# The first pass's rows of an expert layer, turned by a one-hot product instead of a gather

## The chip, the cores and the metric

The kernel runs on one core of one Trainium2 chip. The metric is the device time of one execution in microseconds (us); all arrays are float32 in HBM when it starts. Its engines are TensorE (PE), VectorE (DVE), ScalarE (ACT), GpSimd (POOL) and SyncE (SP, which here only issues DMAs). They run their own instruction streams and meet through semaphores.

## The reference

One inference step of a backbone with two layers over 384 tokens (128 of a prompt, 256 of a sample) of width 1024. Each layer has a mixer and a mixture of 16 experts with 256 hidden columns, of which each token uses two:

```python
scores = jax.nn.sigmoid((t @ router_w).astype(jnp.float32))
sel = scores + router_b.astype(jnp.float32)
grp = sel.reshape(n, N_GROUPS, EXP_PER_GROUP)
gscore = lax.top_k(grp, TOP_K)[0].sum(-1)
g_idx = jnp.argmax(gscore, axis=-1)
...
combine = jnp.sum(jax.nn.one_hot(e_idx, N_EXPERTS, dtype=jnp.float32) * wts[..., None], axis=1).astype(t.dtype)
hid = jax.nn.silu(jnp.einsum('td,edf->tef', t, w1)) * jnp.einsum('td,edf->tef', t, w3)
hid = hid * combine[:, :, None]
return jnp.einsum('tef,efd->td', hid, w2).reshape(bsz, s, d)
```

The mixers (convolution and latent attention in layer 0, spatial gating in layer 1), the adaLN modulation and the norms lie before and between the two expert layers and are not touched.

## The kernel before

**The expert layer.** Every expert j has a fixed stretch of places (`PLACE_AT[j]`, 96, 64 or 32 of them); a token that chooses j takes the next free place of it. The 1152 places are worked off in nine passes of 128. For a pass p the rows of h of its 128 tokens must stand turned (columns of h on the partitions) in `h_slotT`. Then TensorE multiplies them with w1 and w3 of the pass's experts ("up", two halves of 32 products, L1691), ScalarE takes the silu (L725), VectorE multiplies (`gate`), TensorE turns the hidden rows (L1730) and multiplies with w2 ("down", L1706). Down's result goes through y_slot to a table in HBM, from which it is gathered back at the layer's end (L547).

**How a pass got its rows.** In `dispatch` TensorE turns h into rows (L1604), ScalarE copies them to `h_rows` on chip (L764) and stores them in HBM as `h_all` (L767). From the router's scores VectorE makes each token's place in each expert (`place`), compares it with the place numbers 1, 2, ... and so gets a one-hot matrix `chosen` (token by place, fp16; `choose`). TensorE multiplies it with the token numbers and gets the list of tokens by place: `tokens` (L1626), for passes 0 to 2 in `dispatch` and for 3 to 8 later, since the experts from the sixth on are first sorted by their load. VectorE casts the list to the integers `table` (L1102). GpSimd gathers the 128 rows of a pass from `h_all` by the table (`fetch`, L536) into one of two slots of `h_slot`; TensorE turns them (`turn_h`, L1672 and L1676, four transposes each), and ScalarE and VectorE copy the two halves to `h_slotT` (`copy_h`, L721 and L1244). The slots of `h_slot` lie over `h_rows`.

**What sets the order.** Each engine's stream is written out by hand; nothing is scheduled. VectorE's order in `place` is: one-hots of the first four experts and the fifth's stretch of places, the table's cast, the sorting of the experts (`sort_experts`, `order_experts`, which releases the load of the sixth expert's weights on SyncE's queue), the weights of the tokens (`shares`), the modulation columns (`ada`, on which TensorE's experts wait, since it empties a PSUM bank), then in `experts_routed` the later one-hots (`later_places`). TensorE's order in `experts_routed` is:

```python
turn_h(0)
pe.wait_ge(s_chosen, (1 + len(RUNS)) * (l + 1))
tokens(bank[7], *TABLES[1]).then_inc(s_table, 1)
up(0, range(KD // 2))
turn_h(1)
up(0, range(KD // 2, KD))
```

and then the turned weights of the last pass (L1719) and the loop over the passes, in which pass p+1's up stands around pass p's hidden rows and ahead of its down, and `turn_h(p + 2)` between. Weights of six experts are held at a time; SyncE loads an expert's w1 and w3 when the up products of the expert six before it are done, and its w2 after that one's down. PSUM's eight banks are given to the products of `PRODUCTS` in turn.

## Time and profile before

| | us |
|---|---|
| median of 3 runs | 750.0 (749.42 to 752.58) |
| profiled execution | 752.46 |
| its span, first to last instruction | 750.4 |
| TensorE busy | 672.7 |
| VectorE busy | 258.2 |
| ScalarE busy | 159.1 |
| GpSimd busy | 32.5 |

The span is the time from the first instruction of the program to the last; 2.06 us of the execution lie around it. The two expert layers follow at about 262 and 577 us of the span with their dispatch, up of pass 0 starts at 286 and 601, and up of the last pass ends at about 394 and 710. Over the whole span the 16 DMA engines move 285 GB/s; while the passes run it is mostly over 400.

### The profile page before, as it was taken

What the parts mean: (1) busy time and instruction counts of PE and PEld (TensorE: products, weight loads), DVE (VectorE), ACT (ScalarE), POOL (GpSimd) and SP (SyncE); (2) the same over time, 40 slices, a digit from 0 to 9 for tenths busy, and PEclk for the clock granted to TensorE, in tenths of its full rate; (3) what the DMA queues carried; (4) which work ended last, traced back from release to release, by engine and by line L of the source; (5) the groups of instructions that cost most, each with busy time, mean ns of one, the idle gap of its engine ahead of it and who ended that gap; (6) DMA issues with size and microseconds to landing.
All of it is one profiled execution on the core that took longest, in us unless ns stands there. A gap on an engine that the chain in (4) does not pass through costs nothing.

```text
span 750.4 us, 11306 instructions
## 1 busy us (share of the span) xinstructions
PE 672.7 (90%) x4744; PEld 345.0 (46%) x4744; DVE 258.2 (34%) x600; ACT 159.1 (21%) x316; POOL 32.5 (4%) x88
## 2 busy tenths in 40 slices
PE   4699999999989858999977799999998499999884
PEld 2555555557755523333323545556654333333242
DVE  0504678366511473121101620020425711211027
ACT  2301000253411231111111430131013311111023
POOL 2000000000000011000002000000000010010020
PEclk9999999999999987999999999999999889999898
DMA  9996030769974378899997895423745778999852
GB/s 368 381 425 273 33 140 1 317 274 424 424 307 167 131 298 299 324 401 418 425 428 283 324 397 227 183 111 121 314 169 217 290 299 309 405 424 424 352 197 84
DMA packets 27556, 213.63 MB, mean 285 GB/s; under 512 B 2768, under 2 KB 6640, under 8 KB 15856
## 3 DMA queue, kind: packets, MB, share of 16 engines
q1 hardware_dynamic: 17568, 182.06, 59.7%
q0 software_dynamic: 4320, 15.73, 6.0%
q10 hardware_dynamic: 5616, 15.09, 5.1%
q8 instruction: 39, 0.64, 0.3%
q14 instruction: 13, 0.11, 0.0%
HBM read 199.62 MB, written 13.25 MB: 284 GB/s over the span
## 4 chain that ended last, share of the span: by engine, by line
PE 77%; DVE 9%; DMA 8%; issue 2%; ACT 2%; POOL 1%; SPq 0%; POOLq 0%; DVEq 0%; ACTq 0%
PE bank L1447 29%; PE bank L1691 17%; PE bank L1706 8%; PE bank L1784 6%; DMA ring<-in_ada_w 3%; PE bank L1381 2%; DVE work L844 2%; PE bank L1500 2%; DMA state<-y_slots,index 2%; PE bank L1593 2%; DVE xT L847 2%; DMA work<-h_all,table 2%; DVE state L888 1%; PE bank L1672 1%; PE bank L1392 1%
## 5 line engine op out<-in xcount | busy, mean ns | idle before, releaser
L1447 PE MATMUL bank<-state,ring 128*128 128x384 f32 x416 | 136.1, 487 | 1.2 <-ACT state L614 1.2
L1691 PE MATMUL bank<-ring,work 128*32 128x512 f32 x896 | 110.2, 636 | 7.4 <-issue 7.4
L1447 PEld LDWEIGHTS bank<-state,ring 128*128 128x128 f32 x416 | 78.3, 190 | 54.9 <-issue 2.1
L1447 PE MATMUL bank<-work,ring 128*128 128x384 f32 x256 | 83.8, 489 | 0.3 <-DVE work L844 0.3
L1447 PEld LDWEIGHTS bank<-work,ring 128*128 128x128 f32 x256 | 48.6, 191 | 35.1 <-DVE work L844 1.3
L1691 PEld LDWEIGHTS bank<-ring,work 128*32 128x32 f32 x896 | 28.8, 116 | 73.6 <-issue 73.5
L1706 PE MATMUL bank<-ring,work 128*32 128x512 f32 x448 | 50.9, 595 | 2.6 <-ACT work L734 2.6
L1244 DVE COPY work<-bank 128x512 f32<-128x512 f32 x18 | 12.4, 691 | 111.6 <-PE bank L1676 111.6
L847 DVE SCALAR_TENSOR_TENSOR xT<-bank,mod,xT 128x128 f32<-128x128 f32 x64 | 22.5, 411 | 68.4 <-PE bank L1447 67.2
L1784 PE MATMUL bank<-ring,state 128*128 128x512 f32 x96 | 43.3, 612 | 2.4 <-ACT state L614 2.4
L536 POOL DMA_INDIRECT work<-h_all,table x18 | 17.1, 951 | 591.0 <-DMA h_all<-work 455.1
L596 ACT ACTIVATE state<-xT 128x384 f32<-128x384 f32 x40 | 20.6, 522 | 99.2 <-DVE xT L847 88.1
L1418 PE MATMUL bank<-state,share 128*128 128x384 f32 x58 | 22.6, 548 | 10.3 <-ACT state L596 10.3
L1784 PEld LDWEIGHTS bank<-ring,state 128*128 128x128 f32 x96 | 18.7, 196 | 25.7 <-issue 25.2
L1268 DVE COPY work<-bank 128x512 f32<-128x512 f32 x18 | 12.4, 692 | 50.4 <-PE bank L1706 50.4
L1691 PE MATMUL bank<-work 128*32 128x512 f32 x160 | 28.9, 594 | 0.0
L1691 PE MATMUL bank<-state,work 128*32 128x512 f32 x96 | 28.9, 594 | 0.0
L1706 PEld LDWEIGHTS bank<-ring,work 128*32 128x32 f32 x448 | 13.3, 109 | 31.0 <-issue 28.0
L847 DVE SCALAR_TENSOR_TENSOR work<-ring,csil,work 128x768 f32<-128x768 f32 x28 | 26.3, 1011 | 0.0
L1381 PE MATMUL bank<-ring,csil 128*32 128x128 f32 x704 | 22.3, 280 | 4.1 <-DMA ring<-in_ada_w 4.1
L844 DVE TENSOR_TENSOR mod<-bank,smalls 128x8 f32<-128x8 f32 (+1 forms) x32 | 3.8, 158 | 63.3 <-PE bank L1400 63.1
L1672 PE MATMUL bank<-smalls,work 128*128 128x128 f32 x72 | 12.7, 302 | 14.2 <-DMA work<-h_all,table 7.7
(211 smaller groups left out, 724.1 us busy)
## 6 DMA issues: line engine op xcount, KB each, us to landing
ring<-in_moe SPq DMA_DIRECT2D x24, 2048.0 KB, 10.0
ring<-in_ada_w SPq DMA_DIRECT2D x12, 3072.0 KB, 15.1
ring<-in_moe SPq DMA_DIRECT2D x24, 1024.0 KB, 17.9
work<-in_ada_w SPq DMA_DIRECT2D x3, 3072.0 KB, 10.1
work<-in_moe SPq DMA_DIRECT2D x4, 2048.0 KB, 11.6
state<-in_moe SPq DMA_DIRECT2D x4, 2048.0 KB, 14.5
y_slots<-work ACTq DMA_DIRECT2D x16, 512.0 KB, 9.8
ring<-in_gm_in SPq DMA_DIRECT2D x4, 2048.0 KB, 9.0
```

The source lines that it names most:

```text
L536: pool.indirect_dma_start(h_slot[:, p % 2, :], None, h_all, bass.IndirectOffsetOnAxis(ap=table[:, l, p:p + 1], axis=0))\
L596: act.activation(sq[:, k % 4, :], xT[:, k, :], ACT.Square).then_inc(s_sq, 1)
L844: return dve.tensor_tensor(o, x, y, op)
L847: return dve.scalar_tensor_tensor(out=o, in0=x, scalar=s, in1=y, op0=op0, op1=op1)
L1381: mm = pe.matmul(ps[32 * g:32 * g + 32, 0:P], csil[:, k, :], w[:, k, g * P:g * P + P], start=(k == 0), stop=(k == KD - 1))
L1418: mm = pe.matmul(ps[:, 0:T], share[:, n, :], sq[:, sq_at[0] % 4, :], start=(k == 0), stop=(k == tiles - 1))
L1447: mm = pe.matmul(ps[:, 0:T], w[:, k, j * P:j * P + P], x[:, k, :], start=(k == 0), stop=(k == KD - 1))
L1500: mm = pe.matmul(ps[:, 0:T], w_q[:, k, h * P:h * P + P], q_a[:, k, :], start=(k == 0), stop=(k == NQ - 1))
L1672: tr = pe.transpose(bank[2][:, k * P:k * P + P], h_slot[:, b, k * P:k * P + P], ident[:, :])
L1691: mm = pe.matmul(bank[p % 2][rows, :], h_slotT[:, p % 2, k * P + BLOCK * n:k * P + BLOCK * n + BLOCK], held(place_of(e))[:, k * 512:k * 51 ...
L1706: mm = pe.matmul(bank[4 + half][rows, :], hiddenT[:, p % 2, c * P + BLOCK * n:c * P + BLOCK * n + BLOCK], held(place_of(e))[:, at_:at_ + 5 ...
L1784: mm = pe.matmul(ps[:, :], hT[:, k, t * P:t * P + P], w[:, k, :], start=(k == 0), stop=(k == KD - 1))
```

## The change

Pass 0 no longer gathers. VectorE makes a second one-hot matrix for its 128 places, in float32 and on the space of `last_w` (`choose_first`: 96 places of expert 0, 32 of expert 1). TensorE multiplies the rows that still stand in `h_rows` with it (`first_rows`): for each 128 columns of h three products (one for 128 tokens), which give the pass's rows already turned. The eight blocks are made in two halves of 12 products, "hot" 0 and 1, with the first table's products between them, which now are for passes 1 and 2 only. ScalarE copies the first half to `h_slotT`, VectorE the second (`copy_first`, behind the order of the experts, with the table's cast). `h_slotT`'s two slots change places, since slot 0 lies over `h_rows`. The gathers begin with pass 1, and the first waits also for the second half of the products. Up of pass 0 stands ahead of `turn_h(1)` with nothing before it, the later table's products follow pass 0's up, and the last pass's weights are turned after pass 1's up. On VectorE pass 0's gate comes ahead of the later table's cast and the last weights.

```diff
 KEPT = [j for j in range(NE) if PLACE_AT[j] >= STORED]
-TABLES = ((0, PLACE_AT[FIXED] // P), (PLACE_AT[FIXED] // P, PASSES))
+TABLES = ((1, PLACE_AT[FIXED] // P), (PLACE_AT[FIXED] // P, PASSES))
 RUNS = [(4, 1), (5, 2), (7, 1), (8, 8)]
...
     return ([("ada_row", HEAD_ADA[l]), ("router", l), ("logits", l)] + [("h_row", l, t, c) for t in range(NT) for c in range(2)]
-            + [("ada_t", HEAD_ADA[l]), ("slots", l), ("table", l, 0)])
+            + [("ada_t", HEAD_ADA[l]), ("slots", l), ("hot", l, 0), ("table", l, 0), ("hot", l, 1)])
...
         s_kept = carve(NT * len(KEPT))
+        first_hot = last_w
         spare = work[:, work.shape[1] - SLOT:work.shape[1]]
...
                     pool.wait_ge(taken[bank_of(key)[0]], takes(key))
+                    b, turn = bank_of(("hot", l, 1))
+                    pool.wait_ge(full[b], turn + 1)
                 if p == TABLES[1][0]:
                     pool.wait_ge(s_later, l + 1)
-                if p >= 2:
-                    pool.wait_ge(s_turn1[l], p - 1)
+                if p >= 3:
+                    pool.wait_ge(s_turn1[l], p - 2)
                 pool.indirect_dma_start(h_slot[:, p % 2, :], None, h_all,
...
                 pool.wait_ge(s_hstored, 16 * NT * (l + 1))
-                for p in range(PASSES):
+                for p in range(1, PASSES):
                     fetch(l, p)
...
-                act.wait_ge(s_turn0[l], p + 1)
-                act.activation(h_slotT[:, p % 2, 0:512], bank[2][:, :], ACT.Identity).then_inc(s_copy0[l], 1)
+                act.wait_ge(s_turn0[l], p)
+                act.activation(h_slotT[:, (p + 1) % 2, 0:512], bank[2][:, :], ACT.Identity).then_inc(s_copy0[l], 1)
...
             def experts_routed(l):
-                for p in range(2):
-                    copy_h(l, p)
+                take(act.activation(h_slotT[:, 1, 0:512], product("hot", l, 0)[:, :], ACT.Identity), "hot", l, 0)
+                copy_h(l, 1)
                 silus(l, 0)
...
-            def tokens(l):
+            def choose_first(l):
+
+                own = three(s_tmp)
+                for j in range(NE):
+                    if PLACE_AT[j] < P:
+                        first, n = PLACE_AT[j], min(CAPS[j], P - PLACE_AT[j])
+                        places = place_no[:, 0:n].rearrange("p (a n) -> p a n", a=1).to_broadcast([P, NT, n])
+                        tt(first_hot[:, :, first:first + n], places, own[:, :, j:j + 1].to_broadcast([P, NT, n]),
+                           ALU.is_equal).then_inc(s_hot, 1)
+
+            def copy_first(l):
...
                 take(dve.tensor_copy(table[:, l, first:last], product("table", l, 0)[:, 0:last - first]), "table", l, 0)
+                take(dve.tensor_copy(h_slotT[:, 1, 512:D], product("hot", l, 1)[:, :]), "hot", l, 1)
...
                 take(dve.tensor_copy(s_place[:, :], ps[:, 0:NT * NE + NE]), "slots", l)
+                choose_first(l)
                 choose(l, 0, three(s_tmp), (0, 4))
...
                 dve.wait_ge(s_caps, 2 * NE + 1 + SORTED)
-                tokens(l)
                 sort_experts(l)
                 order_experts(l)
+                copy_first(l)
                 shares(l)
...
                 later_places(l)
-                copy_h(l, 0)
+                copy_h(l, 1)
+                gate(l, 0)
                 later_tokens(l)
                 last_weights(l)
-                copy_h(l, 1)
-                gate(l, 0)
-                last_weights_turned(l)
                 for p in range(PASSES):
...
                         copy_h(l, p + 2)
+                    if p == 0:
+                        last_weights_turned(l)
                     if p + 1 < PASSES:
...
+                for t in range(NT):
+                    for c in range(2):
+                        emptied(("h_row", l, t, c))
+                pe.wait_ge(s_hot, 2 * (l + 1))
+                first_rows(l, 0)
                 pe.wait_ge(s_chosen, (1 + len(RUNS)) * l + 1)
                 closed(tokens(opened("table", l, 0), *TABLES[0]), "table", l, 0)
+                first_rows(l, 1)
+
+            def first_rows(l, c):
+
+                ps = opened("hot", l, c)
+                for i in range(4):
+                    for t in range(NT):
+                        k = 4 * c + i
+                        mm = pe.matmul(ps[:, i * P:i * P + P], h_rows[:, t, k * P:k * P + P], first_hot[:, t, :],
+                                       start=(t == 0), stop=(t == NT - 1))
+                closed(mm, "hot", l, c)
...
                     b = p % 2
-                    pe.wait_ge(s_h[l][b], 16 * (p // 2 + 1))
-                    wait(pe, s_copy0[l], p)
+                    pe.wait_ge(s_h[l][b], 16 * ((p + 1) // 2))
+                    wait(pe, s_copy0[l], p - 1)
                     for k in range(4):
...
                     tr.then_inc(s_turn0[l], 1)
-                    wait(pe, s_copy1[l], p)
+                    wait(pe, s_copy1[l], p - 1)
                     for k in range(4, 8):
...
                             pe.wait_ge(ring_full[place_of(e)], 16 * (HOME["moe", (l, e)][1] + 1))
-                        pe.wait_ge(s_copy0[l], p + 1)
+                        if p == 0:
+                            emptied(("hot", l, 0))
+                            emptied(("hot", l, 1))
+                        else:
+                            pe.wait_ge(s_copy0[l], p)
                         wait(pe, s_hid[l], p - 1)
-                    if 4 in tiles:
-                        pe.wait_ge(s_copy1[l], p + 1)
+                    if 4 in tiles and p > 0:
+                        pe.wait_ge(s_copy1[l], p)
                     for k in tiles:
...
                             rows = slice(BLOCK * n, BLOCK * n + BLOCK)
-                            mm = pe.matmul(bank[p % 2][rows, :], h_slotT[:, p % 2, k * P + BLOCK * n:k * P + BLOCK * n + BLOCK],
+                            mm = pe.matmul(bank[p % 2][rows, :], h_slotT[:, (p + 1) % 2, k * P + BLOCK * n:k * P + BLOCK * n + BLOCK],
                                            held(place_of(e))[:, k * 512:k * 512 + 512],
...
-                turn_h(0)
-                pe.wait_ge(s_chosen, (1 + len(RUNS)) * (l + 1))
-                tokens(bank[7], *TABLES[1]).then_inc(s_table, 1)
                 up(0, range(KD // 2))
...
                 up(0, range(KD // 2, KD))
-                pe.wait_ge(s_w8, len(KEPT) * (l + 1))
-                for t in range(NT):
-                    tr = pe.transpose(bank[7][:, P + t * P:P + t * P + P], last_w[:, t, :], ident[:, :])
-                tr.then_inc(s_w8t, 1)
+                pe.wait_ge(s_chosen, (1 + len(RUNS)) * (l + 1))
+                tokens(bank[7], *TABLES[1]).then_inc(s_table, 1)
...
                         up(p + 1, range(KD // 2, KD))
+                    if p == 0:
+                        pe.wait_ge(s_w8, len(KEPT) * (l + 1))
+                        for t in range(NT):
+                            tr = pe.transpose(bank[7][:, P + t * P:P + t * P + P], last_w[:, t, :], ident[:, :])
+                        tr.then_inc(s_w8t, 1)
                     if p + 2 < PASSES:
...
```

The rows below are of the built programs, with the semaphores that an instruction waits for. First TensorE in layer 0, from the first table's products to the second half of pass 0's up, before. `work` is the space in which `h_rows`, `h_slot`, `h_slotT` and the one-hots lie, `smalls` holds the constants, the identity for a transpose and the place numbers among them, `ring` the weights:

```order
L1626 MATMUL bank<-token_h,work 128x1 [waits bank_taken5,chosen_ready]
L1626 MATMUL bank<-token_h,work 128x1 x8
L1672 MATMUL bank<-smalls,work 128x128 [waits bank_taken2,bank_taken3,bank_taken1,bank_taken4,bank_taken0,h_loaded0_0,bank_taken7,bank_taken6]
L1672 MATMUL bank<-smalls,work 128x128 x3
L1676 MATMUL bank<-smalls,work 128x128 x4
L1626 MATMUL bank<-token_h,work 128x1 [waits chosen_ready]
L1626 MATMUL bank<-token_h,work 128x1 x17
L1691 MATMUL bank<-ring,work 32x512 [waits h_copied00,ring_full2,ring_full1]
L1691 MATMUL bank<-ring,work 32x512 x15
L1672 MATMUL bank<-smalls,work 128x128 [waits h_copied00,h_loaded0_1]
L1672 MATMUL bank<-smalls,work 128x128 x3
L1676 MATMUL bank<-smalls,work 128x128 [waits h_copied10]
```

The same place now; L1649 is `first_rows`, L1657 `tokens`, L1726 up, L1703 and L1707 `turn_h`:

```order
L1649 MATMUL bank<-work 128x128 [waits bank_taken1,bank_taken2,bank_taken0,first_places,bank_taken7,bank_taken5,bank_taken6]
L1649 MATMUL bank<-work 128x128 x11
L1657 MATMUL bank<-token_h,work 128x1 [waits bank_taken6,chosen_ready]
L1657 MATMUL bank<-token_h,work 128x1 x5
L1649 MATMUL bank<-work 128x128 [waits bank_taken7]
L1649 MATMUL bank<-work 128x128 x11
L1726 MATMUL bank<-ring,work 32x512 [waits ring_full1,bank_taken4,ring_full2,bank_taken3,bank_taken5,bank_taken2,bank_taken7,bank_taken1,bank_taken0]
L1726 MATMUL bank<-ring,work 32x512 x15
L1703 MATMUL bank<-smalls,work 128x128 [waits h_loaded0_1]
L1703 MATMUL bank<-smalls,work 128x128 x3
L1707 MATMUL bank<-smalls,work 128x128 x4
L1726 MATMUL bank<-ring,work 32x512 x16
```

Up of pass 0 (first with `ring_full`) waited for the copy of a gathered half (`h_copied00`), and now waits for PSUM banks to be emptied (`bank_taken5` and `bank_taken7` are the two halves, `bank_taken3` the modulation). `turn_h(0)` is gone; the eighteen products of the later table have moved behind up.

VectorE in layer 0 from the places of the tokens to the sorting of the experts, before:

```order
L847 SCALAR_TENSOR_TENSOR s_tmp<-bank,s_top 128x48 [waits bank_full4,vector_step]
L1150 COPY s_place<-bank 128x64 [waits vector_step]
L844 TENSOR_TENSOR work<-smalls,s_tmp 128x3x384
L1102 CAST table<-bank 128x3 [waits bank_full5,caps_set,bank_taken4]
L847 SCALAR_TENSOR_TENSOR s_key<-s_place,smalls 128x11
```

And now:

```order
L851 SCALAR_TENSOR_TENSOR s_tmp<-bank,s_top 128x48 [waits bank_full4,vector_step]
L1164 COPY s_place<-bank 128x64 [waits vector_step]
L848 TENSOR_TENSOR work<-smalls,s_tmp 128x3x96
L848 TENSOR_TENSOR work<-smalls,s_tmp 128x3x32
L848 TENSOR_TENSOR work<-smalls,s_tmp 128x3x384
L851 SCALAR_TENSOR_TENSOR s_key<-s_place,smalls 128x11 [waits caps_set,bank_taken4]
```

The two comparisons of 96 and 32 places are new; the table's cast with its wait for TensorE has left this place.

VectorE from the order of the experts to the modulation, before:

```order
L1143 TENSOR_SCALAR order<-order 128x11 [waits vector_step]
L1144 CAST order_i<-order 128x11 [waits vector_step]
L844 TENSOR_TENSOR s_score<-s_score,s_top 128x48
L1084 TENSOR_REDUCE s_den<-s_score 128x3 [waits vector_step]
L1085 RECIPROCAL s_den<-s_den 128x3 [waits vector_step]
L844 TENSOR_TENSOR combine<-s_score,s_den 128x48 [waits vector_step]
L844 TENSOR_TENSOR work<-s_tmp,work 128x363 [waits combine_ready]
L1160 TENSOR_REDUCE work<-work 128x33 [waits vector_step]
L844 TENSOR_TENSOR mod<-bank,smalls 128x8 [waits bank_full3,vector_step]
L844 TENSOR_TENSOR mod<-bank,smalls 128x4
L844 TENSOR_TENSOR mod<-bank,mod 128x4 [waits vector_step]
```

And now:

```order
L1157 TENSOR_SCALAR order<-order 128x11 [waits vector_step]
L1158 CAST order_i<-order 128x11 [waits vector_step]
L1115 CAST table<-bank 128x2 [waits bank_full6]
L1116 COPY work<-bank 128x512 [waits bank_full7]
L848 TENSOR_TENSOR s_score<-s_score,s_top 128x48
L1088 TENSOR_REDUCE s_den<-s_score 128x3 [waits vector_step]
L1089 RECIPROCAL s_den<-s_den 128x3 [waits vector_step]
L848 TENSOR_TENSOR combine<-s_score,s_den 128x48 [waits vector_step]
L848 TENSOR_TENSOR work<-s_tmp,work 128x363 [waits vector_step]
L1175 TENSOR_REDUCE work<-work 128x33 [waits vector_step]
L848 TENSOR_TENSOR mod<-bank,smalls 128x8 [waits bank_full3,vector_step]
L848 TENSOR_TENSOR mod<-bank,smalls 128x4
```

The cast and the copy of the second half (L1116, 512 columns) stand between the order of the experts and the weights of the tokens, each with a wait for TensorE (`bank_full6`, `bank_full7`).

## Rows read from the trace of the kernel before

**Rows 1.** The page, first part: busy us, share of the span, instructions.

```profile
PE 672.7 (90%) x4744; PEld 345.0 (46%) x4744; DVE 258.2 (34%) x600; ACT 159.1 (21%) x316; POOL 32.5 (4%) x88
```

**Rows 2.** Chain of waits, layer 0: start us, us, what the time went to.

```profile
274.72 4.18 DMA h_all<-work
...
280.56 11.55 DMA work<-h_all,table
292.15 0.66 PE bank L1672 x4
293.24 3.57 PE bank L1691 x32
...
381.20 3.79 issue
```

**Rows 3.** Chain of waits, layer 1.

```profile
597.94 2.77 DVE work L844 x4
600.76 0.64 PE bank L1626 x18
601.40 6.25 PE bank L1691 x32
...
608.67 3.57 PE bank L1691 x32
...
696.63 3.64 issue
```

**Rows 4.** VectorE timeline, layer 0: start us, us, instruction, idle before and releaser.

```profile
275.04 1.35 DVE L844 TENSOR_TENSOR work<-smalls,s_tmp 128x1152 f16<-128x1152 f32 x1
276.99 0.16 DVE L1102 CAST table<-bank 128x3 uint32<-128x3 f32 x1 [0.59 <-PE bank L1626]
...
280.26 0.17 DVE L1144 CAST order_i<-order 128x11 int32<-128x11 f32 x1
...
282.67 0.16 DVE L844 TENSOR_TENSOR mod<-bank,mod 128x4 f32<-128x4 f32 x1
282.87 0.46 DVE L844 TENSOR_TENSOR work<-smalls,s_tmp 128x288 f16<-128x288 f32 x1
...
285.78 0.69 DVE L1244 COPY work<-bank 128x512 f32<-128x512 f32 x1 [0.15 <-PE bank L1676]
```

**Rows 5.** TensorE timeline, layer 0.

```profile
283.81 1.09 PE L1672 MATMUL bank<-smalls,work 128*128 128x128 f32 x4 [6.96 <-DMA work<-h_all,table]
...
286.25 5.14 PE L1691 MATMUL bank<-ring,work 128*32 128x512 f32 x32
...
296.75 0.55 PE L1719 MATMUL bank<-smalls,work 128*128 128x128 f32 x3
```

**Rows 6.** Groups of TensorE: count, busy us, mean ns, idle before.

```profile
L1796 PE MATMUL bank<-work 128*128 128x128 f32 x48 | 5.5, 275 | 0.0
```

**Rows 7.** Stretches: us, busy of PE, PEld, DVE, ACT, POOL, granted clock, DMA share, GB/s.

```profile
275.00:276.00 1.00, 0.00 (x0) 0.00 (x0) 1.00 (x2) 0.00 (x0) 0.00 (x0) 0.84 0.75 307
...
289.00:290.00 1.00, 1.00 (x16) 0.19 (x10) 0.00 (x0) 0.00 (x0) 0.00 (x0) 0.83 0.82 344
...
593.00:594.00 1.00, 0.00 (x0) 0.00 (x0) 0.89 (x6) 0.00 (x0) 0.87 (x1) 0.56 0.00 0
...
606.00:607.00 1.00, 1.00 (x8) 0.19 (x4) 0.00 (x0) 0.00 (x0) 0.00 (x0) 0.61 0.97 406
```

**Rows 8.** Timelines of GpSimd in layer 1 and of SyncE's queue in both.

```profile
594.37 0.94 POOL L536 DMA_INDIRECT work<-h_all,table  x1 [0.30 <-issue]
...
281.48 0.36 SPq L459 DMA_DIRECT2D state<-in_moe  x1
...
596.31 0.35 SPq L459 DMA_DIRECT2D state<-in_moe  x1
```

**Rows 9.** Line L536, the gathers of rows of h: from issue to landing.

```profile
DMA to landing us min/median/max: 4.0/10.5/12.8
```

**Rows 10.** DMA issues, stretch 594.3 to 594.6: count, median us to landing.

```profile
work<-h_all,table POOLq DMA_INDIRECT x1, 5.0
```

14 lines of the change are left out of this document (7 added, 7 removed).

## Prediction

> **What bounds the kernel now.** The page's first part is read first: TensorE is busy for nine tenths of the span, and no other engine for more than half [rows 1]. So time is won only where TensorE waits, or where it runs at its lower clock. The chain of waits then shows where it waits near the change. In layer 0 the chain leaves TensorE altogether: the rows of h are stored, the gather of pass 1 is on its way for 11.55 us, and TensorE turns these rows at 292.15; the second half of pass 0's up products starts at 293.24 [rows 2]. In layer 1 the chain goes through VectorE's later one-hot rows, the later table's products and the first half of up, which takes 6.25 us; the second half starts at 608.67 [rows 3]. These two starts, 293.24 and 608.67, are my anchors: behind them pass follows pass without a wait, up to one stop of 3.79 and 3.64 us before the last pass's up products [rows 2, 3]. The chain calls that stop "issue", since a wait for weights is not in its names; the reader should see that a stop ended by a load hides a loss of a few tenths ahead of it, but gives a gain on only if the loads start earlier too.
>
> **VectorE.** Two one-hots of 128x288 and 128x96 stand ahead of the comparison over 1152 columns. The nearest row is the one of 288 columns, 0.46 us [rows 4]; since instructions of this engine overlap a little I put the two at 0.4 and 0.2 (together between 0.5 and 0.9). So the large comparison ends 0.6 later. The wait of 0.59 before the table's cast goes, because the cast moves behind the sorting [rows 4]. The two cancel, and the order of the experts is ready as before (280.43: the cast at 280.26 and its 0.17). Behind it the cast and a new copy of 128x512 come in; the copy of the same shape took 0.69 [rows 4]. The modulation, which ended at 282.83 (282.67 and 0.16), and with it the release of TensorE, come 0.7 later.
>
> **TensorE ahead of the copy.** 24 products of 128x128 by 128 columns are new, 12 in each half. At the full clock 48 products of this shape took 5.5, or 0.115 each [rows 6]: 1.4 for a half. At the lower clock four transposes of the shape took 1.09 [rows 5]: 3.3 at most for a half. In layer 0 the clock fell at 275.7 (0.84 as the mean of 275 to 276, between 1.00 and 0.50, the levels of 2.4 and 1.2 GHz) [rows 7], just where the first half begins (first one-hots at 275.04 + 0.6 = 275.7). I take the first half at the lower level: 275.7 + 3.3 = 279.0; the six table products are put at 0.3 (eighteen took 0.64 [rows 3]). By then the engine has worked for 3.6 us without a pause. The clock rose at 289.3, 5.5 us after work began at 283.81 [rows 5, 7], and in layer 1 at 606.8, 6.0 after 600.76 [rows 3, 7]. So the second half lies between 1.4 and 3.3; I take 1.6, and it ends at 280.9. The copy, which could start at 280.5, waits 0.4 (bounds 0 and 2.1). In layer 1 the clock fell only at 593.1 [rows 7], the products start at 590.7, all are done by 594, and the copy (order ready 595.5) waits for nothing.
> On the price of such a product the Trainium skill differs: "FP8 and Floating Point Precision", section "TensorE Precision Notes", says that true FP32 takes four passes through the array. At 128 columns and 2.4 GHz that is an estimate of 0.21 each, 2.6 a half, and the sum would be about 1 us smaller; the row of 0.115 says about half of that, and it decides.
>
> **The first half of up.** It no longer waits for a gather, nor for the later table. It starts when the modulation is done: 282.83 + 0.7 + 0.4, and a little for the release, 284.0; in layer 1 597.9 + 0.7 + 0.4 = 599.0. The same 32 products take 3.6 at the full level (at 293.24), twice that at half, and took 5.14 and 6.25 here [rows 5, 3]. TensorE stands still from 281 to 284 and from 594 to 599, so I take 6.3 in both: ends 290.3 and 605.3. Turning pass 1 takes 1.1 (292.15 to 293.24). The anchors become 291.4 and 606.4: 1.8 and 2.3 earlier.
>
> **The gather of pass 1.** On POOL's queue it is now the first. It waits for the table's cast, for the second half of the products (its slot lies over the rows they read) and for the stored rows: 280.9 to 281.1 in layer 0 instead of 280.56, 595.8 instead of 594.37 [rows 2, 8]. The load of expert 5 is issued at 281.48 and 596.31 as before [rows 8], since the order of the experts does not move. A gather took from 4.0 to 12.8 [rows 9]; the one issued 1.9 ahead of a load took 5.0 [rows 8, 10], the one 0.9 ahead took 11.55 [rows 2, 8], both behind pass 0's. With nothing ahead of it I take 7: 288 and 603, before 290.3 and 605.3, so no wait. At 12.8 it would be 293.9 and 608.6.
>
> **What moves behind the anchor.** The later table's products, 0.64 [rows 3], now stand after pass 0's up; the three transposes of the last weights, 0.55 [rows 5], move from there to behind pass 1's up. Pass 1's end is 0.1 later against the anchor, later passes 0.6. The stop before the last pass takes up part of it, as long as the loads that end it are released by pass 1 and not by later ones: between 0.1 and 0.6 a layer, I take 0.2. The gather of pass 3 waits for the later table behind pass 0's gate, about 5 us after the anchor instead of 1, and is needed two passes on, at some 12 us each (88 us lie between 293.24 and 381.20, seven and a half passes): hidden even at 12.8. The last weights are needed one pass later than they are ready. SP's queue waits for the same events. ScalarE's new copy of 128x512 lies under the second half of the products.
>
> **Sum.** 1.8 + 2.3 - 0.4 = 3.7 us. The profiled execution took 752.46 (span 750.4 and 2.06 around it) and would take 748.8. The three timed runs have their median at 750.0, so the forecast is 746.3. The bound between "faster" and "no change" is 0.5%, which is 3.75 us and all that a measurement can tell: the forecast stands on it.
>
> **Rivals.**
> A, the clock stays up. If the new products raise the level early and the pause of 3 us does not take it back, the first half of up takes 3.6 in layer 0: it ends 287.6, then waits perhaps 0.4 for the gather, and the anchor is 289.1 instead of 291.4, 2.3 better; in layer 1, with a pause of 5 us and the clock lost after shorter activity, half of that at best. Time 743 to 744. For it: the level in layer 0 rose after 5.5 us of work. Against it: in both layers up began at the lower level, the rise came only at 289.3 and 606.8 [rows 7].
> B, the gather is late though issued first. If the load's data reach the DMA engines while the gather's last rows are still waiting, it takes 11.5 as in layer 0 before: it lands at 292.5 and 607.3, the anchors are 293.5 and 608.3, about as before, and the 0.2 to 0.6 a layer remains. Time 750. For it: its lead over the load shrinks to 0.4 and 0.5 us, where 0.9 was too little before. Against: pass 0's gather, issued just before it, then stood ahead of it in the queue, and now nothing does.
> Here the Trainium skill speaks against the change: "DMA: Bandwidth & Descriptors", section "Queues, rings and completion order", has each DMA engine go round between the queues packet by packet, so that a lead in time protects only what has already moved. The 11.55 agrees with it.
> C, slower. If the second half of the products runs at the lower level to its end, it is done at 282.6, after the load of expert 5 has been issued (281.48): this is the point from which it decides. The copy and the modulation on VectorE wait 2.1, up starts at 285.7, and the gather is issued at 282.7 behind the load and takes 11.5 to 12.8: 294.2 to 295.5. The anchor comes at 295.3 to 296.6, a loss of 2.1 to 3.4. Should the clock fall early in layer 1 too, its products end at 597.6 behind the load at 596.31, and it loses 1.7 to 2.9. Both layers: 754 to 756; layer 0 alone, with layer 1 as forecast: about 751.
> D, the change does what it says at the start, but the stop before the last pass grows by it. If the loads that end the stop leave the DMA engines when they did before, nothing is won: 750. Against: these loads are released by the ends of up, which move with the anchor.
>
> **Chances and range.** The forecast 0.46 (own range 744.5 to 748.5, for the clock's start may cost 1 us either way in each layer), A 0.17, B 0.20, C 0.12 (both layers 0.07), D 0.05. Faster by over 0.5% (below 746.25): half of the forecast and A, with a little from elsewhere: 0.42. Slower (above 753.75): C in both layers, and what runs differ by: 0.11. Within: 0.47. The range leaves out the worse C and the best of A: 742.5 to 752.
>
> **What would show it.** Right: no gather for pass 0; the products from 275.7 and done by 281; up's first half starting near 284 and 599 without a wait for a gather; the second half at 291.4 and 606.4; a stop of about 3.5 before the last pass. The chain in layer 0 should go through VectorE and no longer through a gather. Wrong: a TensorE wait for the DMA before turning pass 1 (B or C); a VectorE wait before the new copy of more than 1 us (C); a stop before the last pass grown by 2 us (D). A level of 1.00 during the first half of up would show A.

## The result, and the profile after

The changed kernel is slower. Its median is 753.27 us (748.84 to 756.47, 20 runs), that of the kernel before, on the same chips, 749.7 us (746.79 to 752.78, 20 runs); the ratio is 1.0059, with a 95% interval of 1.0042 to 1.0075. The forecast was 746.3 in a range of 742.5 to 752.0. The profiled execution took 754.07 us, its span is 752.3 (before: 752.46 and 750.4).

The first fence is the chain of waits of the changed kernel in layer 0, with the stop ahead of the last pass as its last row; columns as in [rows 2].

```profile
276.11 5.46 PE bank L1649 x24
281.71 2.90 PE bank L1649 x24
284.63 0.70 DVE work L1116
285.34 2.71 issue
288.05 5.34 PE bank L1726 x32
...
294.41 3.57 PE bank L1726 x32
...
383.06 3.70 issue
```

The gather of 11.55 us is gone from the chain, as forecast. In its place stand the two halves of the products (L1649), VectorE's copy (L1116) and 2.71 us in which the chain names no releaser. The second half of pass 0's up begins at 294.41; it was 293.24 [rows 2], and 291.4 was forecast.

The next fence is the same view in layer 1, with the stop ahead of the last pass and the end of the layer.

```profile
590.69 2.92 PE bank L1649 x24
593.74 2.80 PE bank L1649 x24
596.60 0.70 issue
597.30 8.92 DMA work<-h_all,table
...
607.36 3.57 PE bank L1726 x32
...
696.08 3.74 issue
...
721.09 1.25 PE bank L1793 x3
722.34 2.60 issue
724.95 6.43 PE bank L1793 x13
```

Here the second half begins 1.3 us earlier than before (607.36 against 608.67 [rows 3]; 606.4 was forecast), and the gather that the change was to hide is on the chain. Counted from the routing's places (the products ahead of the one-hots, which start at 274.44 and 589.02, before at 274.25 and 589.25), the two starts moved by +1.0 and -1.1 us in these executions, where -1.8 and -2.3 were forecast. At the end of the layer TensorE adds the last pass's results (L1793: eight products, which leave sixteen records). It stops after three of the sixteen, for 2.60 us. In the kernel before these sixteen run without a stop, as its timeline has it:

```profile
721.68 7.09 PE L1758 MATMUL bank<-work 128*128 128x384 f32 x16 [2.40 <-issue]
```

VectorE's timeline of the changed kernel in layer 0 answers [rows 4]; the last column is the idle time before and its releaser.

```profile
280.22 0.17 DVE L1158 CAST order_i<-order 128x11 int32<-128x11 f32 x1
281.75 0.16 DVE L1115 CAST table<-bank 128x2 uint32<-128x2 f32 x1 [1.35 <-PE bank L1657]
284.63 0.69 DVE L1116 COPY work<-bank 128x512 f32<-128x512 f32 x1 [2.73 <-PE bank L1649]
...
287.57 0.16 DVE L848 TENSOR_TENSOR mod<-bank,mod 128x4 f32<-128x4 f32 x1
```

The copy stood still for 2.73 us, where 0.4 was forecast and 2.1 was the upper bound. The modulation behind it ends at 287.73; TensorE begins pass 0's up at 288.05. So I read the 2.71 us of "issue" as a wait for VectorE; the run mod_hold below shows it.

The group of the products in the whole program answers [rows 6] (count, busy us, mean ns, idle before), and four stretches answer [rows 7] (the granted clock is the number behind the five busy times).

```profile
L1649 PE MATMUL bank<-work 128*128 128x128 f32 x96 | 14.3, 316 | 2.7 <-DVE work L848 2.7
```

```profile
280.00:281.00 1.00, 1.00 (x7) 1.00 (x6) 0.35 (x2) 0.00 (x0) 0.00 (x0) 0.50 0.00 0
282.00:283.00 1.00, 1.00 (x12) 1.00 (x11) 0.00 (x0) 0.20 (x1) 0.00 (x0) 1.00 1.06 229
289.00:290.00 1.00, 1.00 (x8) 0.27 (x4) 1.00 (x1) 0.00 (x0) 0.00 (x0) 0.50 0.96 406
...
600.00:601.00 1.00, 1.00 (x8) 0.38 (x12) 1.00 (x4) 0.00 (x0) 0.00 (x0) 0.50 1.11 475
```

The change adds 24 products in each of two layers, 48 in all, and the trace has 96 records of them: such a product of float32 leaves two. (So a half of up, called 32 products ahead of the prediction, is 16 products and 32 records: the rows of the built program have 1 and 15 of them, the chain x32. A transpose leaves one: 4 in the program, x4 in the chain.) In layer 0 the first half ran at 0.50 (1.2 GHz), the second at 1.00 (2.4 GHz), and after the pause up's first half began at 0.50 again, in layer 1 too.

Last, the transfers: the issue of expert 5's load on SyncE's queue in layer 0 (it did not move, [rows 8]), then GpSimd's issue of the first gather in layer 0 and in layer 1.

```profile
281.45 0.36 SPq L461 DMA_DIRECT2D state<-in_moe  x1
```

```profile
285.48 1.08 POOL L540 DMA_INDIRECT work<-h_all,table  x1 [280.75 <-PE bank L1649]
...
597.30 0.94 POOL L540 DMA_INDIRECT work<-h_all,table  x1 [183.11 <-PE bank L1649]
```

The gather was to lead the load by 0.4 us; it follows it by 4.0 us in layer 0 and, with the load at 595.78, by 1.5 us in layer 1.

### The profile page after: what moved, and what is told of

Its sections match the earlier page's. It is cut to its first block, busy times and chain, and to the rows that moved or that the text cites. A ratio compares the mean times of both kernels' runs of the same rounds, so it can differ in the third digit from the quotient of the medians.

```text
span 752.3 us, 11460 instructions
## 1 busy us (share of the span) xinstructions
PE 678.7 (90%) x4818; PEld 354.6 (47%) x4818; DVE 259.3 (34%) x604; ACT 158.9 (21%) x316; POOL 30.5 (4%) x86
## 4 chain that ended last, share of the span: by engine, by line
PE 80%; DVE 8%; DMA 6%; issue 3%; ACT 2%; POOL 1%; SPq 0%; DVEq 0%; ACTq 0%; POOLq 0%
PE bank L1462 28%; PE bank L1726 17%; PE bank L1741 8%; PE bank L1819 6%; DMA ring<-in_ada_w 3%; PE bank L1396 2%; PE bank L1515 2%; PE bank L1649 2%; DVE work L848 2%; PE bank L1608 2%; DVE xT L851 2%; DVE state L892 1%; PE bank L1703 1%; DMA work<-h_all,table 1%; PE bank L1564 1%
## 5 line engine op out<-in xcount | busy, mean ns | idle before, releaser
L1726 PE MATMUL bank<-ring,work 128*32 128x512 f32 x896 | 109.1, 630 | 14.6 <-issue 14.5
L1726 PEld LDWEIGHTS bank<-ring,work 128*32 128x32 f32 x896 | 29.6, 115 | 79.4 <-issue 79.4
L1819 PE MATMUL bank<-ring,state 128*128 128x512 f32 x96 | 41.6, 593 | 2.4 <-ACT state L618 2.4
L540 POOL DMA_INDIRECT work<-h_all,table x16 | 15.1, 946 | 591.8 <-PE bank L1649 463.9
L1726 PE MATMUL bank<-work 128*32 128x512 f32 x160 | 28.9, 594 | 0.0
L1726 PE MATMUL bank<-state,work 128*32 128x512 f32 x96 | 28.9, 594 | 0.0
L892 DVE RECIPROCAL state<-state 128x384 f32<-128x384 f32 x6 | 15.3, 2552 | 29.3 <-ACT state L608 29.3
## 6 DMA issues: line engine op xcount, KB each, us to landing
state<-in_moe SPq DMA_DIRECT2D x4, 2048.0 KB, 12.8
y_slots<-work ACTq DMA_DIRECT2D x16, 512.0 KB, 10.3
```

The source lines that it names most:

```text
L540: pool.indirect_dma_start(h_slot[:, p % 2, :], None, h_all, bass.IndirectOffsetOnAxis(ap=table[:, l, p:p + 1], axis=0))\
L892: step(dve.reciprocal(rms, rms))
L1726: mm = pe.matmul(bank[p % 2][rows, :], h_slotT[:, (p + 1) % 2, k * P + BLOCK * n:k * P + BLOCK * n + BLOCK], held(place_of(e))[:, k * 512: ...
L1819: mm = pe.matmul(ps[:, :], hT[:, k, t * P:t * P + P], w[:, k, :], start=(k == 0), stop=(k == KD - 1))
```

## The experiments

Sixteen runs were made, of fifteen kernels (a_pad48r is a_pad48 once more), each timed beside the kernel before. The table that follows is worked out from TensorE's records of each profiled execution. "Front" is the time from the first product of the routing's places (274.25 before) to the first of pass 2's up, in layers 0 and 1; it holds what the change does at a layer's start. "Tail" is the time in layer 1 from the end of the last up to the end of those sixteen records. "Sum" is what front and tail together differ from the kernel before. "Timed" is the ratio less one, with half its 95% interval, times 749 us.

```
kernel          front 0  front 1   tail    sum     timed us
before            34.97    35.39  18.23      0            0
changed           36.32    34.70  21.41   +3.8   +4.4 +-1.2
third             35.92    35.64  18.20   +1.2   +2.5 +-1.9
act_copy          39.63    38.03  18.06   +7.1   +9.1 +-2.2
hold              35.29    33.28  20.27   +0.3   +1.6 +-2.0
mod_hold          33.08    33.19  20.89   -1.4   -2.3 +-1.9
mod_late          35.45    34.49  21.53   +2.9   +4.1 +-1.6
mod_hold_late     31.00    32.36  21.13   -4.1   -4.6 +-2.0
b_moved           32.75    33.62  18.16   -4.1   -2.7 +-2.2
b_pad76           35.68    35.16  21.49   +3.7   +4.5 +-1.6
b_pad124          33.96    34.95  23.69   +4.0   +3.7 +-1.8
a_pad48           37.20    34.84  18.27   +1.7   +5.5 +-1.8
a_pad48r          37.23    34.77  22.55   +6.0   +5.2 +-2.0
a_pad176          37.13    35.19  24.77   +8.5   +7.7 +-2.4
a_lead            36.55    35.88  18.13   +2.0   +1.9 +-1.9
best48            30.31    30.31  23.79   -4.2   -0.5 +-2.0
best176           31.09    30.31  25.09   -2.1   -0.6 +-1.8
best_lead         30.95    30.32  18.20   -9.1   -3.6 +-1.5
```

The column "sum" follows "timed" within about 2 us, but for a_pad48 and for best48 and best_lead, of which more below. Front and tail are of one execution each, and executions differ: the kernel before and its two paddings (b_pad76, b_pad124), whose fronts are the same code, have 33.96 to 35.68 in layer 0 and 34.95 to 35.39 in layer 1; the changed kernel and a_pad48, a_pad48r, a_pad176 and a_lead have 36.32 to 37.23 and 34.70 to 35.88. Smaller differences than these say nothing. By the means of these two groups the change costs 2.0 us in layer 0 and nothing in layer 1 (34.9 and 36.9, 35.2 and 35.1); the tail, 3.2 us longer, is the larger part of the loss.

**third: the products made cheap.** In first_rows only one of three products of each tile is left:

```
-  for t in range(NT):
-      mm = pe.matmul(..., h_rows[:, t, ...], first_hot[:, t, :], start=(t == 0), stop=(t == NT - 1))
+  mm = pe.matmul(..., h_rows[:, 0, ...], first_hot[:, 0, :], start=True, stop=True)
```

> The changed kernel with 4 products a half instead of 12: only the first 128 tokens' rows are multiplied, the other tokens of pass 0 get zeros (that part of the computation is left out). Theory P (two TensorE instructions for each float32 product, so 24 a half, 5.5 us at the lower clock and 2.9 at the full one): both halves are done by 281, VectorE's copy waits under 1 us, the gather is issued ahead of or beside expert 5's load at 281.5, and the second half of up starts at about 291.4 and 606, as forecast: 747 to 748.5 us with the stop in the last addition, 746 without. If the products are not what holds VectorE, its copy still waits over 2 us and the time stays above 752.

Measured 750.24 us (12 runs), ratio 1.0033 (1.0007 to 1.0059), more than the 746 to 748.5 expected. The gather in the chain of this kernel in both layers, then TensorE's timeline at the turning:

```profile
280.12 11.57 DMA work<-h_all,table
...
594.30 11.39 DMA work<-h_all,table
```

```profile
291.74 0.66 PE L1702 MATMUL bank<-smalls,work 128*128 128x128 f32 x4 [3.36 <-DMA work<-h_all,table]
...
605.73 0.66 PE L1702 MATMUL bank<-smalls,work 128*128 128x128 f32 x4 [3.21 <-DMA work<-h_all,table]
```

Up began 9.33 us after the routing's places in both layers, 2.7 us sooner than before, and TensorE then waited for the gather, 6.6 us over both layers. The gather went out within 0.2 us of the load and took 11.4 to 11.6. The fronts (35.92 and 35.64) are no shorter than the kernel before's. So cheap products would not have given the forecast either: rival B's mechanism was there. The tail has no stop here; this program is also shorter, of which more below.

**act_copy: the copy taken off VectorE.** ScalarE copies the second half of the first rows.

```
+  take(act.activation(h_slotT[:, 1, 512:D], product("hot", l, 1)[:, :], ACT.Identity), "hot", l, 1)
-  take(dve.tensor_copy(h_slotT[:, 1, 512:D], product("hot", l, 1)[:, :]), "hot", l, 1)
```

> The changed kernel, with the second half of pass 0's turned rows copied by ScalarE instead of VectorE. Theory C (the copy blocks VectorE): up of pass 0 starts when ScalarE's copy is done, near 285.4 instead of 288.05 in layer 0 and near 598 instead of 599.97 in layer 1, the second half of up follows 2 us earlier in each, 749 us. Theory G (the gather is the second limit): up starts as early, but TensorE then waits for the gather, issued at 285.5 and landing at 292.6 as before, and the second half moves by 0.7 and 0 us: 752.5 us, less 2.6 if the code behind layer 1's If happens to lie better.

Measured 758.93 us (6 runs), ratio 1.0121 (1.0092 to 1.015). TensorE's timeline of this kernel in layer 0:

```profile
285.71 3.64 PE L1726 MATMUL bank<-ring,work 128*32 128x512 f32 x32 [0.78 <-ACT work L733]
294.28 1.12 PE L1703 MATMUL bank<-smalls,work 128*128 128x128 f32 x4 [4.93 <-DMA work<-h_all,table]
295.19 1.06 PE L1707 MATMUL bank<-smalls,work 128*128 128x128 f32 x4
296.18 5.23 PE L1726 MATMUL bank<-ring,work 128*32 128x512 f32 x32
```

Up began 11.15 us after the routing's places in place of 13.61, and at the full level (3.64); then TensorE stood 4.93 us for the gather, and what follows ran at half the clock (turning 1.12 and 1.06 in place of 0.66 and 0.60, the second half of up 5.23 in place of 3.64). Both expectations, 749 and 752.5, were too low: theory G had the wait, but not the low level behind it. Here an earlier start that ended in a wait was worse than a later one.

**hold: the load made to wait.** Expert 5's load waits for the gather.

```
   sp.wait_ge(s_order, l + 1)
+  sp.wait_ge(s_h[l][1], 16)
   load_up(l, FIXED)
```

> The changed kernel, with expert 5's load on SyncE made to wait until pass 1's gather has landed. Contention theory (the load's packets hold back the gather's): the gather, 7.14 us in layer 0 and 8.92 in layer 1 of the changed kernel, takes 4.0 to 5.5 as the two did in layer 1 of the kernel before; layer 0 gains nothing by it, since nothing waits for the gather there, and layer 1 gains the 1.35 us of TensorE's wait, so the time falls by 1 to 2 us (about 752). Rival (the gather is slow by itself, for what its table or rows are): 7 to 9 us as before, and no gain. Second rival: the load, 8 to 10 us later, is late for pass 3 or lies on the next gathers, and the time rises by over 1 us.

Measured 750.75 us (12 runs), ratio 1.0022 (0.9995 to 1.0049). The gather of layer 1 in this kernel (issues, count, median us to landing), layer 0 being the same with 4.4:

```profile
work<-h_all,table POOLq DMA_INDIRECT x1, 4.3
```

7.14 and 8.92 us became 4.4 and 4.3: the load is what slows the gather. The later load delayed nothing that shows, and the time lies 1.6 us above the kernel before in place of 4.4. The front of layer 0 is 1.0 us shorter too, where nothing was expected; there the first half of the products took 4.55 us in place of 5.46, as it also did in some executions without this edit (4.29 in a_pad48r).

**mod_hold, mod_late, mod_hold_late.** In all three VectorE's copy of the second half stands behind the modulation; "hold" is the edit above; "late" turns pass 1's rows behind six of pass 0's eight tiles.

```
-  take(dve.tensor_copy(h_slotT[:, 1, 512:D], ...), "hot", l, 1)      # in copy_first
...
   ada(HEAD_ADA[l])
+  take(dve.tensor_copy(h_slotT[:, 1, 512:D], product("hot", l, 1)[:, :]), "hot", l, 1)
...
-  up(0, range(KD // 2))
+  up(0, range(6))
   turn_h(1)
-  up(0, range(KD // 2, KD))
+  up(0, range(6, KD))
```

> The changed kernel, with VectorE's copy of the second half of the first rows moved behind the shares and the modulation, and expert 5's load held until pass 1's gather has landed. Theory (the products cost 2.9 us a half, and the modulation, 2.4 us that stood behind the copy, is what TensorE waited for): pass 0's up begins at about 285.7 and 597.7 in place of 288.05 and 599.97, and with a gather of 4 to 5.5 us its second half begins at 290 to 291.5 and 602.5 to 604 in place of 294.4 and 607.3; some 5 to 7 us less than the changed kernel: 746 to 748. Rival (what stands behind the copy is not what TensorE waits for): up begins where it does now, 752 to 753. Rival on the clock: a wait for the gather, however short, keeps the engine at its low level through the next stretch and half of the gain goes: 749 to 751.

> The changed kernel, with VectorE's copy of the second half moved behind the modulation, and the turning of pass 1's rows moved from behind four of pass 0's eight tiles to behind six; expert 5's load stays where it is. Theory (gather and load collide; the gather takes 8 to 8.5 us as it did where ScalarE made the copy): up begins at about 285.7 and 597.7, six tiles take 5.4 to 7 us, the gather lands at 294 and 606, and TensorE waits for it 1.5 to 3 us in each layer: 750 to 754, below the 758.9 of the kernel with ScalarE's copy, whose wait was 4.4 to 4.9. Rival (the loss in that kernel came of the copy on ScalarE and not of the wait): 747 or less.

> The last two together: the copy behind the modulation, the load held, the turning behind six tiles. Theory: no wait for the gather is left (4 to 5.5 us from about 285.8, six tiles from 285.7 end at 291 to 292.7); pass 0's up ends 4 to 5 us earlier than in the changed kernel, and 1 to 3 us earlier than in the kernel before: 744 to 748. If code placement is what made the changed kernel slower, 750 or more, with the early ends given back at a stop.

Measured: mod_hold 747.21 us, ratio 0.9969 (0.9943 to 0.9994); mod_late 753.83, 1.0055 (1.0033 to 1.0077); mod_hold_late 744.94, 0.9939 (0.9913 to 0.9964), the kernel before at 748.55; all three lie in the ranges expected. TensorE's timeline at the first half of up in layer 0, in the changed kernel and then in mod_hold:

```profile
288.05 5.34 PE L1726 MATMUL bank<-ring,work 128*32 128x512 f32 x32 [3.45 <-issue]
```

```profile
284.71 3.64 PE L1727 MATMUL bank<-ring,work 128*32 128x512 f32 x32 [0.94 <-DVE work L1177]
```

Between the products and up TensorE stood 3.45 us in both layers of the changed kernel and 0.94 in both of mod_hold (3.48 and 3.45 with the load held alone): the modulation behind VectorE's copy is what it had waited for. The chain of mod_hold_late in layer 0:

```profile
277.00 4.46 PE bank L1650 x24
281.58 2.80 PE bank L1650 x24
284.47 0.70 DVE work L1177
285.31 5.36 PE bank L1727 x48
...
291.69 1.85 PE bank L1727 x16
294.08 3.57 PE bank L1727 x32
```

Products, copy, six tiles of up at the full level, turning, two tiles: no wait for VectorE's modulation and none for a gather is left. Pass 1's up begins 18.75 us after the routing's places (275.33); in the kernel before it was 23.05 (297.30 in its chain). In mod_late, without the held load, TensorE still waits 5.7 us for the gathers over both layers and nothing is won: the gather is the second limit, as the theory had it, and the wait is where the gain of the first edit goes.

**b_moved: the moves alone.** The kernel before, with the later table's products behind pass 0's up, the last weights' transposes behind pass 1's up, and VectorE's copies and first gate ahead of the later table's cast; pass 0's rows are still gathered.

```
-  tokens(bank[7], *TABLES[1]).then_inc(s_table, 1)
   up(0, range(KD // 2))
   turn_h(1)
   up(0, range(KD // 2, KD))
+  tokens(bank[7], *TABLES[1]).then_inc(s_table, 1)
```

> The kernel before, with only the moves of the change: the later table's products behind pass 0's up, the last weights' transposes behind pass 1's up, and VectorE's copies and the first gate ahead of the later table's cast. My prediction priced these moves at -0.4 us over both layers. From the changed kernel's stages: pass 1 (from its up to pass 2's up) grows from 11.99 to 12.32 us by the transposes, pass 0's up begins 0.6 to 1.9 us earlier without the products' 0.64 us and their wait for VectorE, and its second half still waits for the gather in layer 0. So 747 to 749, no change by more than 1 us. Rival (the moves are what makes the changed kernel slow): 750 or more. Second rival (the later gather, issued later since the table's cast is later, is late for pass 2): a wait at pass 2's turning, 750 or more.

Measured 745.74 us (12 runs), ratio 0.9964 (0.9935 to 0.9993): better than expected, and not to be told from the best version with products (-2.7 +-2.2 against -4.6 +-2.0). The load was not held in a kernel without products, so whether the products add anything to the moves and the held load is not shown. The fronts of before, changed, b_moved and mod_hold_late as stretches (length; busy of PE, PEld, DVE, ACT, POOL; granted clock, DMA share, GB/s):

```profile
274.25:309.22 34.97, 25.36 (x223) 9.89 (x226) 14.20 (x44) 4.62 (x8) 4.83 (x5) 0.80 0.72 269
```

```profile
274.44:310.76 36.32, 31.50 (x259) 16.71 (x263) 14.75 (x46) 4.61 (x8) 3.89 (x4) 0.86 0.64 245
```

```profile
276.65:309.40 32.75, 24.37 (x222) 9.73 (x226) 14.27 (x44) 4.61 (x8) 4.98 (x5) 0.84 0.75 287
```

```profile
275.33:306.33 31.00, 28.70 (x260) 15.29 (x263) 14.64 (x46) 4.60 (x8) 4.97 (x4) 0.94 0.64 248
```

The changed kernel's TensorE is busy for 6.1 us more than before in this stretch and 7.1 more than with the moves alone. In b_moved's layer 0 the gather of pass 1 also went out 2.2 us ahead of the load instead of 0.9, and landed in 5.1 in place of 11.55; this lead differs between executions of one front (0.7 in b_pad76, 1.6 in b_pad124), so part of the 2.2 us won in layer 0 may be chance, and is not shown to be the moves. In layer 1, where the gather was early before as well, 1.8 us are won: pass 0's up no longer waits for the later one-hots and the later table's products (2.77 and 0.64 us in the chain [rows 3]).

**b_pad76, b_pad124, a_pad48, a_pad48r, a_pad176: code that is never run.** So many transposes are put into the branch of layer 1 that is not taken, in the kernel before (b) or the changed one (a):

```
   pe.wait_ge(s_grow[l], 16 * NT)
+  for _ in range(76 if l == 1 else 0):
+      pe.transpose(bank[0][:, 0:P], all_rows[:, 0, 0:P], ident[:, :])
```

> The kernel before, with 76 transposes (some 152 instructions, as many as the change adds in all) in the body of layer 1's If on TensorE, which is not taken. Theory L: the code behind the If now lies as in the changed kernel, a stop of 2 to 3 us appears among the last addition's products in layer 1, and the time is 752.3 (ratio 1.003). If it lies otherwise than counted, no stop and 749.7. Theory P: no stop, 749.7, ratio 1.000.

> The kernel before, with 124 transposes in the branch of layer 1 that is not taken, in place of the 76 that brought the stop and 752.4 us: the code behind the branch lies about where it does in the changed kernel with 48. Theory (the stop decides): the last addition takes 7.1 us and the time is that of the kernel before, within 1 us. Rival (code length or placement costs time in another way than by this stop): the addition takes 7.1 us and the time stays over by 2 to 4 us. Second rival (the stop is there at any length): the addition takes 10 us, 751 to 753.

> The changed kernel, with 48 more transposes in the body of layer 1's If on TensorE, which is not taken: nothing more is executed, but the code behind the If lies elsewhere. Theory L (code layout): the stop of 2.60 us after the third product of the last addition in layer 1, beside which the trace shows a 16 KB load of instructions, is a wait for code; it goes or moves, and the kernel takes some 2.5 us less than the changed one, about 751 (ratio to before 1.002 or 1.003). Theory P (products): the stop is something else and the price is that of the products alone; the stop stays, time 753.3, ratio 1.005 or more.

> The changed kernel with 48 transposes there, once more. Theory (its one profiled execution missed a stop that most of its executions have): a profile with a stop of 3 to 6 us between the last up and the end of the last addition, and a time of 753 to 755 as before. Rival (it has no stop, and its time was high for another reason): again 18.3 us from the last down's up to the end of the addition, and a time that is 753 or more. Third: no stop, and about 751, the first timing being off.

> The changed kernel with 176 transposes in the branch of layer 1 that is not taken. Theory (a program that jumps past the branch meets a stop or none by where the code lies; 76 more than before, 124 more and 80 more brought stops of 2.6 to 5.5 us, none more brought none, and a load of instructions is 16 KB, which I take to be 256 instructions from the number of records between two loads): with about 256 more than before the stops are gone, the last addition takes 7.1 us behind a wait of about 2.5, the span is 2.5 to 3 us shorter and the time is 750 to 751. Rival (placement is not what costs): the time stays at 753 to 754.

Measured: 752.44, 751.96, 754.53, 754.04 and 755.43 us; the ratios are in the table. The theories of b_pad76 and a_pad48r came out, those of the other three did not. The end of layer 1 in b_pad76, then in b_pad124, then in a_pad176:

```profile
720.56 1.66 issue
722.22 1.21 PE bank L1760 x3
723.43 2.53 issue
725.96 6.69 PE bank L1760 x13
```

```profile
714.18 5.97 issue
720.16 8.31 PE bank L1760 x16
```

```profile
715.65 7.78 issue
723.43 7.59 PE bank L1795 x16
```

Instructions that nobody runs bring b_pad76 the changed kernel's stop, after the same three records, and cost the kernel before 4.5 and 3.7 us (b_pad76, b_pad124). With more of them the stop stands at the jump itself, and the chain's "issue" there grows to 6 and 8 us. My expectation of a period (a third place without a stop at 176) was wrong. That a longer jump costs more is not shown: in time b_pad124 does not lie above b_pad76, nor best176 (below) above best48, and only a_pad176 lies above its neighbours. In a_pad48 the profiled execution had no stop; it took 752.12 us where the median is 754.53, and in the same kernel's repeat, a_pad48r, the stop was there (tail 22.55). So executions of one kernel differ in it.

What the stop waits for can be read from the transfers. All eleven profiles with a stop have a load of 16 KB of instructions between the last down and the end of the stop. Whether the stop lasts 0.48 us (hold) or 2.64 (mod_late), TensorE goes on 2.2 to 2.8 us after this load begins (hold: load at 718.19, on at 720.65; changed kernel: 722.70 and 724.95; b_pad124: 717.32 and 720.16), or 4.5 us after it where two loads run at once (a_pad176, best176). In the profiles without a stop the load begins while the last down still runs (a_pad48, act_copy), or only behind the third record, where it holds up nothing (kernel before: 723.31). So TensorE waits for code. Why it has the next code in hand in one kernel or execution and not in another, the runs do not show.

**a_lead: the whole code shifted.** 208 waits on a semaphore that is up already stand ahead of TensorE's first norm, beside the first load.

```
+  for _ in range(208):
+      pe.wait_ge(s_ones, 1)
   norm(0)
```

> The changed kernel with 208 waits on a semaphore that is already up put ahead of TensorE's first norm (while the first 23 us load is on its way), so that its code is 16 KB longer than that of the kernel before and lies as it does, in the places of layer 1 at least. Theory (placement against the 16 KB pieces in which code is loaded brings the stop): from the end of the last up to the end of the last addition 18.2 us as before, in place of 21.4, and 750 to 751 in place of 753.3. Rival (the stop comes of something else, or goes to the branch of layer 0): 753 to 754, with the stop at the addition of one layer or the other.

Measured 750.59 us, ratio 1.0026 (1.0001 to 1.0052). The end of layer 1:

```profile
719.02 1.71 issue
720.72 7.01 PE bank L1795 x16
```

The stop is gone from the profile without a change to what the kernel does. The time is 2.5 us below the changed kernel's (+1.9 +-1.9 against +4.4 +-1.2), which is little more than the two intervals allow (2.3).

**best48, best176, best_lead.** mod_hold_late with 48 and 176 transposes in the branch, and with the 208 waits.

> The kernel with the copy behind the modulation, the load held and the turning behind six tiles (744.94 us), with 48 transposes put into the branch of layer 1 that is not taken. Theory (the stop of about 2.6 us in the last addition is a matter of where the code lies): the last addition takes 7.1 us in place of 10.0, as it did in the changed kernel with the same 48, the span is 2.5 to 3 us shorter, and the time is 741.5 to 743. Rival (the stop is made up for elsewhere, since the changed kernel's time did not fall with it): 744 to 746 with the short addition in the profile.

> The kernel with the copy behind the modulation, the load held and the turning behind six tiles, with 176 transposes in that branch. Theory: no stop, last addition 7.1 us with a wait of about 2.5 ahead of it, 741 to 742.5, against 744.94 without and 747.4 with 48. Rival: 744 to 747.

> The kernel with the copy behind the modulation, the load held and the turning behind six tiles, and the same 208 waits at the start. Theory: the last addition takes 7.1 us in place of 10.0, 741.5 to 743 (744.94 without). Rival: 744 to 747.

Measured 747.4, 747.39 and 745.79 us; ratios 0.9993 (0.9966 to 1.002), 0.9992 (0.9969 to 1.0016) and 0.9952 (0.9932 to 0.9971). All three were expected lower (741 to 743). The paddings cost 4 us, about as in the kernel before. The waits took the stop out of the profile (tail 18.20, span 741.3), but the median is no lower than mod_hold_late's, and the profiled execution is the fastest of its twelve (743.13). Of that kernel's ten runs and this one's twelve only one each was profiled, so how often the stop comes, how often layer 1 starts at the high clock as in these three profiles (front 30.3, where mod_hold_late has 32.36), and so what the stop costs in the median, stays open.

## Why the prediction was wrong, point by point

- **What bounds the kernel** held: what differs lies in the two fronts and, unforeseen, in the tail.
- **TensorE ahead of the copy** is the first step that failed. A half was priced at 1.4 us at the full clock and 3.3 at half; it took 2.9 and 5.5. I read 48 records [rows 6] as 48 products, but a float32 product has two records, so the row's 5.5 us are 24 products at 0.23. The bound of 3.3 was taken from transposes [rows 5], which have one record each, and is no measure for a product either. By the four passes that the Trainium skill gives for true FP32 ("FP8 and Floating Point Precision", "TensorE Precision Notes") the estimate was 0.21, and the runs, with 2.80 us for 12 products at the full level, agree with it. I had sided with the misread row.
- **VectorE**: its own part held, the order of the experts was ready at 280.39 (forecast 280.43). The copy's wait, taken as 0.4 and 0, was 2.73 and 1.52, because the products ended at 284.6 and 596.5 and not at 280.9 and 594. All of the modulation stood behind it, and TensorE behind that: up at 288.05 and 599.97, not 284.0 and 599.0. mod_hold's edit took this away (0.94 us between products and up in place of 3.45).
- **The gather of pass 1** is the second step that failed. It was to go out ahead of the load and take 7. It went out behind it, so that rival C's point was passed in both layers, though by the products' size and, in layer 1, without a low clock. third shows that the 7 was wrong for what I had assumed: sent nearly level with the load (0 and 0.15 us ahead, where 0.4 and 0.5 were assumed) it takes 11.4 to 11.6. So products as cheap as I took them would still have met a wait for the gather (3.36 and 3.21 us in third). In the changed kernel the load's head start brought it down to 7.14 and 8.92, close to the 7 by luck.
- **The first half of up** ran at the low level first, 5.34 and 4.94 us where I had 6.3. This error took back 1.0 and 1.4 us of the late start, by luck. Where the products ran faster and up began earlier (a_pad48r: 12.33 us after the routing's places instead of 13.61), the front of layer 0 was no shorter (37.23): the first half took 6.54, the gather 9.98, and TensorE waited for it.
- **What moves behind the anchor**: the transposes lengthen pass 1 from 11.99 to 12.32 us in every kernel that has the move, where 0.55 was priced. But the moves win time at the front: alone they give 2.7 us (+-2.2), where the whole change was to give 3.7. Against b_moved the products cost the changed kernel 3.6 and 1.1 us in the fronts.
- **What was not in the sum**: the tail, 3.2 us in the profiled execution and the larger part of the loss against the kernel before. It is a wait for code (b_pad76, a_lead, and the loads of instructions); in the median the paddings cost the kernel before 3.7 and 4.5 us, and taking the stop away won 2.5 in a_lead and nothing in best_lead. No step of mine priced code that becomes longer.
- **Rivals**: A was not seen in the changed kernel (up's first half began at the low level in both layers); in act_copy and mod_hold up did run at the full level (3.64). D was not seen either (stops of 3.70 and 3.74 before the last pass, 3.79 and 3.64 before [rows 2, 3]). B's mechanism was shown by third. C's point of decision (the products done after the load has been issued) was passed in both layers, but not at C's price: in layer 0 the anchor came 1.2 us later where C had 2.1 to 3.4, in layer 1 it came 1.3 earlier where C had 1.7 to 2.9 later, and the gather took 7.14 and 8.92 and not 11.5 to 12.8. That the time came out near C's 754 to 756 is owed to the tail, which C does not have.

## What to carry to other kernels

Before a row's mean is taken as the price of an operation, count how many records one operation of the program leaves. When a wait is shortened, list what the next wait would be and run the change with both taken away: here the copy taken off VectorE alone was a loss, the held load alone showed no gain over the kernel before, the copy behind the modulation with the later turning won nothing, and all together gave 4.6 us (+-2.0). And time the moves that come with an idea by themselves; here they alone gave 2.7 us (+-2.2), and what the idea adds to them is not shown.

## What was not expected of the hardware

- Pass 1's gather of 128 rows took 4.3 to 5.7 us in the kernels that hold the load of expert 5 (2 MB and, 0.5 us later, 1 MB), and 5.0 to 5.5 with a lead of 1.9 to 2.2 us over it. With a lead of 1.6 it took 10.3, with 0 to 0.9 it took 11.4 to 11.9. (With a lead of 0.7 to 2.2 pass 0's gather stood just ahead of it.) Sent 1.5 us behind the load it took 8.9 to 10.1, 2.8 to 2.9 behind 9.8 to 10.0, and 3.1 to 4.3 behind 7.1 to 8.5. The longest were those level with the load or less than 1 us ahead of it.
- Behind a jump over code that is not run TensorE stopped, for 0.5 to 2.6 us among the first products or for some 4 to 6 us more than the usual 2.4 at the jump, and it went on 2.2 to 2.8 us after a load of 16 KB of instructions had begun (4.5 after two at once). The Trainium skill says that a taken branch whose target is outside the window of two pages forces a fetch before execution goes on ("Runtime: NRT & Kernel Launch", "Instruction fetch mechanics"); the padded kernels agree with it, and put the price at these figures.
- After a wait of 4.9 us for a gather TensorE ran at half its clock through the turning and half a pass's up (act_copy), so that the wait cost more than its own length. It did so too after 4.37 us (act_copy, layer 1) and after 2.69 (mod_late, layer 1), but after 3.36 and 3.21 (third) and 3.05 (mod_late, layer 0) it ran on at the full level.
